# A diffusion-transformer step on one core: expert rows accumulated by DMA in two DRAM tensors, the last tile placed by TensorE

## Chip, core and metric

The kernel runs on one core of one Trainium2 chip. The metric is device time of one launch in microseconds (us); lower is better. Before the change it is 1660.75 us, the median of three runs (1660.02 to 1660.82).

## What is computed

Two layers of a transformer with shared router, over 640 tokens (128 context, 512 latent) of width 1024, all in float32. Each layer has modulation, a combined input projection, two kinds of attention, merge and output projection, and then a mixture of experts. The change touches the last part and the start of what follows it:

```python
    combine = jnp.sum(jax.nn.one_hot(idx, N_EXPERTS, dtype=jnp.float32) * w[..., None], axis=-2)
    out = jnp.zeros_like(h)
    for e in range(N_EXPERTS):
        hid = jax.nn.silu(h @ w_gate[e]) * (h @ w_up[e])
        out = out + combine[..., e:e + 1] * (hid @ w_down[e])
...
    x = x + gt2 * moe(h2, lp['w_router'], lp['b_router'], lp['w_gate'], lp['w_up'], lp['w_down'])
```

Every token goes to two of the 16 experts (`idx` has two entries), so there are 1280 pairs of token and expert. `gt2` is a row of 1024 values, one for context tokens and one for latent tokens. The next layer begins with an RMS norm of the new `x`.

## The kernel before

**Tiles.** The 1280 expert rows are sorted on the chip into 18 tiles of 128 slots: ten full tiles (one expert each, 128 slots) and eight pair tiles (two experts, 64 slots each). Slots that get no row stay empty, and a pair tile may be empty altogether. The order is fixed in `SCHED` (L67 to L70): tiles 0 and 1 are full, then pair and full tiles alternate (2 is a pair, 3 full, and so on), 15 and 16 are full and 17 is the last pair tile.

**One tile.** TensorE (PE) multiplies the gathered rows with the gate and up weights (`gate_up`, L2200), ScalarE (ACT) applies silu, VectorE (DVE) makes `hid` (L1758), PE transposes it and multiplies it with the down weights into two PSUM banks (`down`, L2233). `ys` (L1170 on ACT, L1724 on DVE) scales one bank each by the slot's routing weight into `ysb`, of which there are two buffers. The loop over tiles is software-pipelined: on PE `gate_up(n)`, then the transposes of the rows of n+1, then `down(n-1)`, then the transposes of `hid` of n. Full tiles from 2 on are computed in three passes, for which ACT makes `hi` and DVE `lo` parts of weights and rows (L1161, L1715, L1720). `gate_up(n+1)` waits for `hid(n)` and, in a full tile, for both `lo` parts of its rows.

**Queues.** SP issues the loads of full tiles' weights. GpSimd (POOL) issues, in one fixed order and into one software queue, the gathers of rows (`xg`, L795), the weights of pair tiles (`gu_a`, `gu_b` with 2 MB each, L804; `dn_a`, `dn_b` with 512 KB each, L811) and the scatter of results (`store_rows`, L827): each slot of `ysb` goes to its own row of `ye_d` in DRAM, 1280 rows, empty slots being skipped (`oob_is_err=False`). `ys(n)` waits until the store of tile n-2 has landed (`y_stored`, L1728), since it writes the same buffer.

**After the last tile.** `load_back` (L604) waits for all stores, then loads for each token tile the two rows of every token (`Y1`, `Y2`); `x` and the gate rows `gt` have been loaded before that (`rows_return`, L591). DVE does three passes of 128x1024 per token tile (L1357, L1361, L1365): sum of the two, times gate, plus `x`. At the end of the kernel each tile is stored to `y_out` (L672). Between the layers the same passes alternate with the norm of the next layer (L1389 to L1398): mean square, inverse root, then PE transposes, ACT and DVE modulate and split (`head_evac`, `head_half`, `head_lo`), and PE starts its first projection tile by tile. PE runs 13 matmuls without a use (`keep_busy`, L1986, L1988) around that point.

Of the kernel before, what the change touches and what calls it, by code (L numbers as in the profile page):

```python
# [24 lines left out]
P = 128  # L25
D = 1024
# [111 lines left out]
def program(nc, w_stream, w_gu, w_dn, x_in, c_cols, params, b_mod2, vecs, g_norm2, da_kc, da_vc, na_kc, na_vc, na_bias,  # L138
            w_router, b_router, consts, rc_in, tok_in, rope, y_out, dk_out, dv_out, nk_out, nv_out):
    nc.disable_value_cache = True  # L140
    ctx = ExitStack()
    with ctx:
# [56 lines left out]
        tok = at("tok", [P, 2 * NT], F32)  # L199
# [112 lines left out]
        def in_junk(name, shape, dt, kb):  # L312
# [6 lines left out]
        row_t = in_junk("row_t", [P, 2 * NT, MOE_TILES], F16, 1)  # L319
        w_rest = in_junk("w_rest", [P, 2 * NT], F32, 1.75)  # L320
        w_tab = [in_hi("w_tab0", [P, 2 * NT, MOE_TILES], F16, 16), in_hi("w_tab1", [P, 2 * NT, MOE_TILES], F16, 16.5),
                 in_junk("w_tab2", [P, 2 * NT, MOE_TILES], F16, 0.5)]
# [17 lines left out]
        ye_d = nc.dram_tensor("ye_d", [2 * NT * P, D], F32, kind="Internal").ap()  # L340
# [122 lines left out]
        inv_ready = Signal("inv_ready", 1)  # L463
        etab_ready = Signal("etab_ready", 1)
        eidx_ready = Signal("eidx_ready", 1)
# [11 lines left out]
        y_act = Signal("y_act", MOE_TILES)  # L477
        y_dve = Signal("y_dve", MOE_TILES)
        y_stored = [Signal(f"y_stored{b}", half[b], 0, 16) for b in range(2)]
        gathered = [Signal(f"gathered{t}", 5 if t == 0 else 3, 0, 16) for t in range(NT)]  # L480
# [27 lines left out]
        s_out = sem("out_stored")  # L508
# [45 lines left out]
        def _(sp):  # L554
# [9 lines left out]
            for l in range(DEPTH):  # L564
# [26 lines left out]
                def rows_return(l):  # L591
                    for k in range(MU):
                        sp.wait_ge(*unit_used(l, N_FULL - 2, k))
                    sp.wait_ge(dn_used.sem, dn_used.at(l, N_PAIR - 2))
                    sp.wait_ge(x_parked.sem, x_parked.at(l, 0))
                    sp.wait_ge(mod_stored.sem, mod_stored.at(l, 3))
                    for t in range(NT):
                        sp.dma_start(x[:, t, :], x_spill[:, t, :]).then_inc(gathered[t].sem, 16)
                        if t == 0:
                            for cond in range(2):  # L600
                                sp.dma_start(gt[:, cond, :], mod_d[l, cond, 5 * D:6 * D].partition_broadcast(P)
                                             ).then_inc(gathered[0].sem, 16)
# [9 lines left out]
                for u in range(NU):  # L612
# [3 lines left out]
                    if l >= 1 and u == 3:  # L616
                        rows_return(l - 1)
# [1785 lines left out]
```

## Time and profile before

| what | value |
|---|---|
| runs timed without the profiler | 1660.02, 1660.75, 1660.82 us |
| profiled execution, first to last instruction (span) | 1665.8 us |
| PE busy | 1550.5 us, 93% of the span |
| DVE busy | 899.4 us, 54% |
| ACT busy | 700.1 us, 42% |
| POOL busy | 297.8 us, 18% |
| mean granted TensorE clock | 0.974 of full speed |
| chain that ended last | 81% PE, 8% DMA, 6% DVE |
| moved by DMA | 337.55 MB, mean 203 GB/s |

The profiled execution has only its span as a time of its own; it is 5.05 us longer than the median of the three runs. A busy share is an average over stages with different limits. The expert stage runs from about 622 to 825 us in the first layer and from about 1435 to 1636 us in the second; the tail after it ends at 1665.8 us.

### The profile page before, as it was taken

The numbers are of one execution on the slowest core, as the hardware profiler recorded it, in microseconds if no ns is written. First come the engines' busy times: TensorE is split into PE (matmuls) and PEld (weight loads), VectorE is DVE, ScalarE is ACT, GpSimd is POOL, SyncE is SP. The second block draws the span as 40 slices with busy tenths as digits, with TensorE's granted clock in tenths as the row PEclk, the third lists the DMA queues.
The fourth block names the chain that finished last, engine by engine and source line by source line (L and its number), as shares of the span: only waits on it lengthen the run. The fifth ranks groups of instructions, "written<-read, shape, count | busy, mean of one in ns | idle before, by whom it ended". The sixth has DMA issues, their size and how long they took to land.

```text
span 1665.8 us, 21787 instructions
## 1 busy us (share of the span) xinstructions
PE 1550.5 (93%) x8180; PEld 1107.1 (66%) x8180; DVE 899.4 (54%) x1723; ACT 700.1 (42%) x1335; POOL 297.8 (18%) x321
## 2 busy tenths in 40 slices
PE   4999999999999989999779999999999999899992
PEld 1777777777787855554456777777777888555561
DVE  1566664455554752455575656543455556344554
ACT  4543554445521313444553455534454132144550
POOL 1001000011101014565200010000111010345640
PEclk9999999999999989999989999999999999999996
DMA  8541205534365379999847212353345253898847
GB/s 339 205 153 58 77 26 189 185 109 161 111 234 219 135 278 400 383 401 346 303 178 270 95 39 77 120 185 126 114 152 204 87 202 127 308 414 336 331 143 286
DMA packets 92376, 337.55 MB, mean 203 GB/s; under 512 B 20960, under 2 KB 21024, under 8 KB 89328
## 3 DMA queue, kind: packets, MB, share of 16 engines
q1 hardware_dynamic: 53136, 197.68, 32.5%
q0 software_dynamic: 38992, 135.86, 22.1%
q10 hardware_dynamic: 144, 2.62, 0.4%
q8 instruction: 65, 1.06, 0.3%
q14 instruction: 39, 0.32, 0.1%
HBM read 351.22 MB, written 47.35 MB: 239 GB/s over the span
## 4 chain that ended last, share of the span: by engine, by line
PE 81%; DMA 8%; DVE 6%; ACT 2%; issue 2%; SPq 1%; POOL 0%; POOLq 0%; ACTq 0%; DVEq 0%
PE ps L1884 16%; PE ps L1886 16%; PE ps L1885 16%; PE ps L2214 6%; PE ps L1876 5%; DMA gu_b<-w_gu,eidx 4%; PE ps L2263 3%; PE ps L2036 3%; PE ps L2018 2%; PE ps L1843 2%; PE ps L1792 2%; PE ps L2096 2%; PE ps L2197 2%; PE ps L2230 2%; PE ps L2070 1%
## 5 line engine op out<-in xcount | busy, mean ns | idle before, releaser
L1884 PE MATMUL ps<-hi,hT_hi 128*128 128x512 f32 x960 | 392.8, 409 | 5.5 <-ACT o_a L1094 3.0
L1886 PE MATMUL ps<-hi,hT_lo 128*128 128x512 f32 x960 | 377.1, 393 | 0.0
L1885 PE MATMUL ps<-lo,hT_hi 128*128 128x512 f32 x960 | 376.3, 392 | 0.0
L1884 PEld LDWEIGHTS ps<-hi,hT_hi 128*128 128x128 f32 x960 | 181.8, 189 | 64.8 <-issue 23.6
L1886 PEld LDWEIGHTS ps<-hi,hT_lo 128*128 128x128 f32 x960 | 181.4, 189 | 40.1
L1885 PEld LDWEIGHTS ps<-lo,hT_hi 128*128 128x128 f32 x960 | 182.2, 190 | 32.4
L890 ACT ACTIVATE hi<-raw 128x1024 fp32r<-128x1024 f32 x106 | 108.4, 1054 | 136.6 <-DMA raw<-w_stream 136.6
L1236 DVE TENSOR_TENSOR lo<-raw,hi 128x1024 fp32r<-128x1024 f32 x106 | 127.5, 1220 | 65.4 <-ACT hi L890 65.0
L1715 DVE TENSOR_TENSOR lo<-raw,hi 128x1024 fp32r<-128x1024 f32 x96 | 112.7, 1221 | 39.7 <-ACT hi L1161 33.9
L2214 PE MATMUL ps<-gu_a,xT 128*64 128x512 f32 x256 | 116.1, 607 | 6.7 <-DMA gu_b<-w_gu,eidx 6.7
L2214 PE MATMUL ps<-gu_b,xT 128*64 128x512 f32 x256 | 116.1, 607 | 0.0
L1161 ACT ACTIVATE hi<-raw 128x1024 fp32r<-128x1024 f32 x96 | 95.5, 1055 | 5.0 <-PE ps L1886 5.0
L1071 ACT ACTIVATE e_da<-ps,neg_m 128x640 f32<-128x640 f32 (+1 forms) x80 | 55.9, 704 | 73.2 <-DVE neg_m L1493 73.2
L2214 PEld LDWEIGHTS ps<-gu_a,xT 128*64 128x64 f32 x256 | 34.5, 140 | 74.7 <-issue 74.7
L1493 DVE TENSOR_REDUCE neg_m<-ps 128x1 f32<-128x640 f32 (+1 forms) x80 | 53.7, 712 | 54.3 <-PE ps L2025 38.4
L1758 DVE TENSOR_TENSOR hid<-ps,silu_g 128x256 f32<-128x256 f32 x36 | 15.3, 424 | 124.1 <-ACT silu_g L1187 107.0
L1351 DVE TENSOR_REDUCE ssum<-sq 128x8 f32<-128x512 f32 x40 | 27.4, 685 | 78.4 <-ACT stg L988 78.4
L1187 ACT ACTIVATE silu_g<-ps 128x256 f32<-128x256 f32 x36 | 13.8, 383 | 131.0 <-PE ps L1886 58.2
L987 ACT ACTIVATE sq<-ps 128x512 f32<-128x512 f32 x40 | 23.9, 597 | 104.5 <-PE ps L1886 104.5
L927 ACT ACTIVATE pT_na<-ps 128x384 f32<-128x384 f32 (+1 forms) x80 | 31.8, 446 | 77.0 <-PE ps L1876 77.0
L2263 PE MATMUL ps<-dn_a,hidT 128*64 128x512 f32 x128 | 60.0, 612 | 3.2 <-ACT hidT L1195 1.7
L830 POOL DMA_INDIRECT ye_d<-ysb,row_i x36 | 50.7, 1409 | 65.9 <-DVE ysb L1732 57.5
(312 smaller groups left out, 2880.8 us busy)
## 6 DMA issues: line engine op xcount, KB each, us to landing
raw<-w_stream SPq DMA_DIRECT2D x112, 512.0 KB
raw<-w_gu SPq DMA_DIRECT2D x80, 512.0 KB
raw_m<-w_stream SPq DMA_DIRECT2D x68, 512.0 KB, 5.4
raw<-w_dn SPq DMA_DIRECT2D x40, 512.0 KB
bias_na<-na_bias POOLq DMA_DIRECT2D x32, 384.0 KB, 3.4
sg<-sg_d POOLq DMA_DIRECT2D x8, 1280.0 KB, 9.7
y<-ye_d SPq DMA_DIRECT2D x20, 512.0 KB, 5.2
raw_p<-w_stream SPq DMA_DIRECT2D x16, 512.0 KB, 16.0
```

Of the source, the lines that this page charges most:

```text
L890: act.activation(hi[s][:], raw[s][:], ACT.Copy).then_inc(is_hi.sem, 1)
L1071: act.activation(e_da[:, i % 2, m, 0:nk], ps_flat[:, m * 1024:m * 1024 + nk], ACT.Exp, bias=neg_m[:, 2 * (i % 2) + m:2 * (i % 2) + m + 1], ...
L1161: act.activation(hi[k][:], raw[w][:], ACT.Copy).then_inc(is_hi.sem, 1)
L1236: dve.tensor_tensor(lo[s][:], raw[s][:], hi[s][:].bitcast(F32), ALU.subtract).then_inc(is_lo.sem, 1)
L1493: dve.tensor_reduce(neg_m[:, c:c + 1], ps_flat[:, m * 1024:m * 1024 + nk], AX.X, ALU.max, negate=True).then_inc(mx_done.sem, 1)
L1715: dve.tensor_tensor(lo[w][:], raw[w][:], hi[k][:].bitcast(F32), ALU.subtract).then_inc(is_lo.sem, 1)
L1876: ins = pe.transpose(ps[:, 5 + n % 2, j * P:(j + 1) * P], src, ident[:])
L1884: pe.matmul(out, w_hi, m_hi, start=first, stop=False)
L1885: pe.matmul(out, w_hi, m_lo, start=False, stop=False)
L1886: return pe.matmul(out, w_lo, m_hi, start=False, stop=last)
L2214: ins = pe.matmul(ps[cs, 0, :], xT[:, kc, cs], pair_gu[q % 2][h][:, kc * 512:(kc + 1) * 512], start=(kc == 0), stop=(kc == KC - 1))
L2263: ins = pe.matmul(ps[cs, 2 + c, :], hidT[:, k, cs], pair_dn[q % 2][h][k][:, c * 512:(c + 1) * 512], start=(k == 0), stop=(k == 1))
```

## The change

There are now two DRAM tensors per layer, `acc[l][0]` and `acc[l][1]`, each with 640 token rows and 128 spare rows. The first is filled with `x` (the store that went to `x_spill`), the second with zeros (`zero_in`, five stores from POOL during attention). POOL adds each tile's `ysb` to one of them with an indirect DMA that accumulates (`compute_op=ALU.add`): full tiles in turn to one or the other, a pair tile's first 64 slots to the first and its last 64 to the second. Every add waits until the add before it on the same tensor has landed (`added`). Empty slots are added to spare rows, so each add moves all its rows.

The gate is applied before the add: DVE writes the gate row of each slot into `ysb` (`row_gates`, one pass of 128x1024, placed ahead of `hid(n)` and waiting for the adds of two tiles before), and `ys` multiplies both PSUM banks by weight and gate on DVE (two passes of 128x512). ACT has no part in it. The gate rows are loaded before the expert stage.

The last tile is not added by DMA. DVE builds five 128x128 matrices of zeros and ones (`perm`), PE multiplies each with the last `ysb` (two matmuls per token tile), and DVE adds the two banks to `x`. `load_back` therefore waits for the adds of tiles 0 to 16 alone, and loads `x` and `xb` for each token tile: one DVE pass of 128x1024 and two of 128x512 per token tile instead of three of 128x1024. At the start of the second layer these passes are ordered differently, the 13 matmuls without a use are gone, and the scratch for DMA descriptors is half of its default (`dynamic_dma_scratch_size=8192`), which makes room for the gate rows.

```diff
+LAST = MOE_TILES - 1
+ACC_ROWS = (NT + 1) * P
+ADD_TO = {}
+for _n in range(LAST):
+    ADD_TO[_n, 0] = SCHED[_n][1] % 2 if IS_FULL[_n] else 0
+    if not IS_FULL[_n]:
+        ADD_TO[_n, 1] = 1
+ADD_NO = {key: sum(1 for other in ADD_TO if other < key and ADD_TO[other] == b) for key, b in ADD_TO.items()}
...
-                def rows_return(l):
+                def load_back(l):
                     for k in range(MU):
                         sp.wait_ge(*unit_used(l, N_FULL - 2, k))
...
+                    for b in range(2):
+                        sp.wait_ge(added[b].sem, added[b].at(l, N_ADDS[b] - 1))
                     for t in range(NT):
...
+                        sp.dma_start(x[:, t, :], acc_x[l][:, t, :]).then_inc(x_loaded[t].sem, 16)
+                        sp.dma_start(xb[t][:], acc[l][1][t * P:(t + 1) * P, :]).then_inc(x_loaded[t].sem, 16)
...
-                def store_rows(n):
-                    po.wait_ge(y_act.sem, y_act.at(l, n))
+                def add_part(n, h):
+                    b = ADD_TO[n, h]
+                    if ADD_NO[n, h] >= 1:
+                        po.wait_ge(added[b].sem, added[b].at(l, ADD_NO[n, h] - 1))
+                    rows_at = row_h if h else row_i
+                    p1 = P if IS_FULL[n] else HALF
+                    po.indirect_dma_start(acc[l][b], bass.IndirectOffsetOnAxis(rows_at[0:p1, XD_COL[n]:XD_COL[n] + 1], 0),
+                                          ysb[n % 2][h * HALF:h * HALF + p1, :], None, bounds_check=ACC_ROWS - 1,
+                                          oob_is_err=True, compute_op=ALU.add).then_inc(added[b].sem, 16)
...
-                def ys(n):
+                def row_gates(n):
+
                     if n >= 2:
-                        dve.wait_ge(y_stored[n % 2].sem, y_stored[n % 2].at(l, n // 2 - 1))
+                        for h in range(1 if IS_FULL[n - 2] else 2):
+                            b = ADD_TO[n - 2, h]
+                            dve.wait_ge(added[b].sem, added[b].at(l, ADD_NO[n - 2, h]))
...
+                    return chained(STT(out=ysb[n % 2][:], in0=gtm[:, 0, :], scalar=p_slot[:, c:c + 1], in1=gtm[:, 1, :],
+                                       op0=ALU.mult, op1=ALU.add))
...
+                def ys(n, gated):
+
+                    dve.wait_ge(*down_done(l, n))
+                    after(gated)
...
+                        ins = STT(out=half_row, in0=ps[:, 2 + j, :], scalar=w_slot[:, c:c + 1], in1=half_row, op0=ALU.mult,
+                                  op1=ALU.mult)
...
+                    if n >= 1:
+                        gated = row_gates(n - 1)
                     dve.wait_ge(silu_done.sem, silu_done.at(l, n))
                     dve.tensor_tensor(hid[:], ps[:, 0, D_EXP:2 * D_EXP], silu_g[:], ALU.mult).then_inc(hid_done.sem, 1)
...
+                def last_rows(l, t):
+                    dve.wait_ge(x_loaded[t].sem, x_loaded[t].at(l, 1))
+                    after(chained(dve.tensor_tensor(x[:, t, :], x[:, t, :], xb[t][:], ALU.add)))
+                    dve.wait_ge(pm_done.sem, pm_done.at(l, t))
+                    for j in range(2):
+                        half_row = x[:, t, 512 * j:512 * j + 512]
+                        ins = dve.tensor_tensor(half_row, ps[:, PERM_BANKS[t][j], :], half_row, ALU.add)
+                    ins.then_inc(x_ready.sem, 1)
...
+                    ins = pe.matmul(ps[:, PERM_BANKS[t][j], :], perm[:, t, :], ysb[LAST % 2][:, 512 * j:512 * j + 512],
+                                    start=True, stop=True)
```

**VectorE, tile 4 (a pair tile) and its neighbours, before.** `ysb_93` is the buffer of odd tiles, the first row of the fence is `hid` of tile 4, and `y_stored1` counts landed stores of odd tiles.

```order
L1715 TENSOR_TENSOR lo_59<-raw_58,hi_60 128x1024 [waits w_hi]
L1758 TENSOR_TENSOR hid<-ps,silu_g 128x256 [waits silu_done]
L1720 TENSOR_TENSOR xT_lo<-ps,xT_hi 128x512 [waits xt_act] x2
L1732 TENSOR_SCALAR ysb_93<-ps,w_slot 128x512 [waits y_stored1,w_used11]
L1758 TENSOR_TENSOR hid<-ps,silu_g 128x256 [waits silu_done]
```

**The same place after.** `rows_added0` and `rows_added1` count landed adds on the two tensors.

```order
L1728 TENSOR_TENSOR lo_59<-raw_58,hi_60 128x1024 [waits w_hi]
L1746 SCALAR_TENSOR_TENSOR ysb_95<-gtm,p_slot 128x1024 [waits rows_added1]
L1794 TENSOR_TENSOR hid<-ps,silu_g 128x256 [waits silu_done]
L1733 TENSOR_TENSOR xT_lo<-ps,xT_hi 128x512 [waits xt_act] x2
L1756 SCALAR_TENSOR_TENSOR ysb_95<-ps,w_slot,ysb_95 128x512 [waits dve_chain,w_used11]
L1756 SCALAR_TENSOR_TENSOR ysb_95<-ps,w_slot,ysb_95 128x512
```

The wait for tile 1's result to have left the buffer stood behind `hid` and the two `xT_lo`; now it stands ahead of them.

**GpSimd, from tile 1's result on, before.** The names are those of the text above.

```order
L804 DMA gu_a_240<-w_gu,eidx 128x4096 [waits pair_gu_used]
L830 DMA ye_d<-ysb_93,row_i 1280x1024 [waits y_dve,y_act]
L795 DMA xg_250<-h_d,inv_i 128x1024 [waits xt_done]
L811 DMA dn_b_70<-w_dn,eidx 128x1024 [waits pair_dn_used]
L830 DMA ye_d<-ysb_251,row_i 1280x1024 [waits y_dve,y_act]
L804 DMA gu_b_241<-w_gu,eidx 128x4096 [waits pair_gu_used]
```

**The same place after.**

```order
L815 DMA gu_a_251<-w_gu,eidx 128x4096 [waits pair_gu_used]
L844 DMA acc_1<-ysb_95,row_i 768x1024 [waits y_dve]
L806 DMA xg_261<-h_d,inv_i 128x1024 [waits xt_done]
L822 DMA dn_b_70<-w_dn,eidx 128x1024 [waits pair_dn_used]
L844 DMA acc_0<-ysb_262,row_i 768x1024 [waits rows_added0,y_dve]
L844 DMA acc_1<-ysb_262,row_h 768x1024 [waits rows_added1]
L815 DMA gu_b_252<-w_gu,eidx 128x4096 [waits pair_gu_used]
```

Tile 2's result is now two DMAs, and the second waits until tile 1's add has landed; `gu_b` of pair tile 6 stands behind that wait.

## Rows read from the trace of the kernel before

**Rows 1.** The page: busy time of PE, and the chain that ended last

```profile
PE 1550.5 (93%) x8180; PEld 1107.1 (66%) x8180; DVE 899.4 (54%) x1723; ACT 700.1 (42%) x1335; POOL 297.8 (18%) x321
...
PE 81%; DMA 8%; DVE 6%; ACT 2%; issue 2%; SPq 1%; POOL 0%; POOLq 0%; ACTq 0%; DVEq 0%
```

**Rows 2.** Windows (us): busy PE, PEld, DVE, ACT, POOL; granted clock; DMA share; GB/s

```profile
660.00:688.00 28.00, 26.39 (x131) 14.14 (x129) 13.88 (x17) 14.87 (x24) 14.91 (x12) 1.00 1.02 421
1470.00:1505.00 35.00, 31.33 (x145) 17.01 (x145) 14.32 (x18) 15.31 (x24) 16.99 (x15) 0.95 1.02 419
```

**Rows 3.** Timeline of POOL: start, length, instruction, idle before and its releaser

```profile
658.23 1.01 POOL L830 DMA_INDIRECT ye_d<-ysb,row_i  x1 [0.30 <-issue]
...
669.04 1.98 POOL L804 DMA_INDIRECT gu_b<-w_gu,eidx  x1 [0.31 <-issue]
...
1471.03 1.02 POOL L830 DMA_INDIRECT ye_d<-ysb,row_i  x1 [0.30 <-issue]
```

**Rows 4.** Timeline of DVE: `hid` of tile 4 and `ys` of tile 3, both layers

```profile
672.50 0.42 DVE L1758 TENSOR_TENSOR hid<-ps,silu_g 128x256 f32<-128x256 f32 x1
...
678.73 0.75 DVE L1732 TENSOR_SCALAR ysb<-ps,w_slot 128x512 f32<-128x512 f32 x1 [4.16 <-DMA ye_d<-ysb,row_i]
...
1485.25 0.42 DVE L1758 TENSOR_TENSOR hid<-ps,silu_g 128x256 f32<-128x256 f32 x1
...
1492.82 0.75 DVE L1732 TENSOR_SCALAR ysb<-ps,w_slot 128x512 f32<-128x512 f32 x1 [5.49 <-DMA ye_d<-ysb,row_i]
```

**Rows 5.** Timeline of PE: `gate_up` of tiles 5 and 6; then one of PE's waits (second layer)

```profile
675.83 0.48 PE L1884 MATMUL ps<-hi,xT_hi 128*128 128x512 f32 x1
...
688.90 1.08 PE L2214 MATMUL ps<-gu_a,xT 128*64 128x512 f32 x1 [2.51 <-DMA gu_b<-w_gu,eidx]
...
1488.57 0.48 PE L1884 MATMUL ps<-hi,xT_hi 128*128 128x512 f32 x1
...
1504.73 0.61 PE L2214 MATMUL ps<-gu_a,xT 128*64 128x512 f32 x1 [1.78 <-DMA gu_b<-w_gu,eidx]
...
PE ps L2263 <- DMA dn_b<-w_dn,eidx: 1.5, 1, 1.5
```

**Rows 6.** Tiles 10 to 12 of the first layer: DVE and PE timelines

```profile
740.62 0.42 DVE L1758 TENSOR_TENSOR hid<-ps,silu_g 128x256 f32<-128x256 f32 x1
...
743.98 0.75 DVE L1732 TENSOR_SCALAR ysb<-ps,w_slot 128x512 f32<-128x512 f32 x1 [1.28 <-DMA ye_d<-ysb,row_i]
...
756.95 1.09 PE L2214 MATMUL ps<-gu_a,xT 128*64 128x512 f32 x1 [2.42 <-DMA gu_b<-w_gu,eidx]
```

**Rows 7.** A quiet cycle, DVE and PE; lines of DVE with min/median/max ns

```profile
1576.44 0.42 DVE L1758 TENSOR_TENSOR hid<-ps,silu_g 128x256 f32<-128x256 f32 x1
...
1579.76 0.48 PE L1884 MATMUL ps<-hi,xT_hi 128*128 128x512 f32 x1
...
L1289 DVE SCALAR_TENSOR_TENSOR hrow<-x,nr,G x10: 1283/1285/1286, 560.8 to 1401.8; 128x1024 f32<-128x1024 f32 x10
...
L1604 DVE TENSOR_TENSOR x<-x,tmp x20: 691/692/694, 548.8 to 1399.1; 128x512 f32<-128x512 f32 x20
```

**Rows 8.** The chain that ended last, its end, and `ys` of tile 16

```profile
1631.07 0.75 DVE L1732 TENSOR_SCALAR ysb<-ps,w_slot 128x512 f32<-128x512 f32 x1 [2.09 <-PE ps L1886]
...
1637.39 2.10 DMA ye_d<-ysb,row_i
...
1639.92 4.46 DMA y<-ye_d
1644.41 1.24 DVE y L1357
...
1661.54 1.23 DVE x L1365
```

**Rows 9.** DVE between the layers: first row sum and last `hT_lo`

```profile
835.71 1.23 DVE L1357 TENSOR_TENSOR y<-y,y 128x1024 f32<-128x1024 f32 x1 [3.68 <-DMA y<-ye_d]
...
882.37 1.29 DVE L1346 TENSOR_TENSOR hT_lo<-y,hT_hi 128x512 fp32r<-128x512 f32 x2 [0.40 <-ACT hT_hi L972]
```

More of the change, by code:

```diff
@@ L339, in program @@
         sg_d = nc.dram_tensor("sg_d", [len(GATES), NT, P, 512], F32, kind="Internal").ap()
-        ye_d = nc.dram_tensor("ye_d", [2 * NT * P, D], F32, kind="Internal").ap()
+        acc = [[nc.dram_tensor(f"acc{l}_{b}", [ACC_ROWS, D], F32, kind="Internal").ap() for b in range(2)]
+               for l in range(DEPTH)]
+        acc_x = [a[0][0:NT * P, :].rearrange("(t p) d -> p t d", p=P) for a in acc]
         ps = ctx.enter_context(nc.psum_tensor("ps", [P, 8, 512], F32))
@@ L476, in program @@
         ht_lo = Signal("ht_lo", sum(IS_SPLIT))
[L477 to L480, printed above, removed]
+        y_dve = Signal("y_dve", LAST + 3)
+        added = [Signal(f"rows_added{b}", N_ADDS[b], 0, 16) for b in range(2)]
+        settled = Signal("acc_zeroed", NT, 0, 16)
+        gtm_loaded = Signal("gtm_loaded", 2, 0, 16)
+        pm_done = Signal("pm_done", NT)
+        x_loaded = [Signal(f"x_loaded{t}", 2, 0, 16) for t in range(NT)]
         x_ready = Signal("x_ready", NT)
@@ L642, in _ @@
                 head_pair(3)
+                sp.wait_ge(mod_stored.sem, mod_stored.at(l, 3))
+                for cond in range(2):
+                    sp.dma_start(gtm[:, cond, :], mod_d[l, cond, 5 * D:6 * D].partition_broadcast(P)
+                                 ).then_inc(gtm_loaded.sem, 16)
                 def weights(j, units):
@@ L671, in _ @@
                 sp.wait_ge(x_ready.sem, x_ready.at(DEPTH - 1, t))
-                sp.dma_start(y_out[:, t, :], x[:, t, :]).then_inc(s_out, 16)
-            sp.wait_ge(s_out, 16 * NT)
+                sp.dma_start(y_out[:, t, :], x[:, t, :]).then_inc(x_parked.sem, 16)
+            sp.wait_ge(x_parked.sem, x_parked.layer * DEPTH + 16 * NT)
         @blk.gpsimd
@@ L734, in _ @@
                     store_gate(g)
+                    if 2 <= g < 2 + NT:
+                        r0 = (g - 2) * P
+                        po.dma_start(acc[l][1][r0:r0 + P, :], zero_in).then_inc(settled.sem, 16)
                 po.wait_ge(kv_out.sem, kv_out.at(l, 1))
@@ L1751, in _ @@
                     head_rows(l + 1)
+                dve.wait_ge(gtm_loaded.sem, gtm_loaded.at(l, 1))
+                after(chained(TT(gtm[:, 0, :], gtm[:, 0, :], gtm[:, 1, :], ALU.subtract)))
                 for n in range(MOE_TILES):
@@ L1778, in _ @@
                             next_lo(w)
-                ys(MOE_TILES - 1)
+                ys(LAST, row_gates(LAST))
                 if l + 1 < DEPTH:
@@ L1965, in head_unit @@
                 def head_unit(k, t):
+                    if k == 0 and t < 2 and l >= 1:
+                        pe.wait_ge(x_ready.sem, x_ready.at(l - 1, 3 + t))
                     if k == 0:
```

174 lines of the change are left out of this document (92 added, 82 removed).

## Prediction

> **What bounds the kernel.** I read the page first: PE is busy for 93% of the span and makes up 81% of the chain that ended last, so time moves only where PE waits or has nothing left to do [rows 1]. Then the windows of the expert stage, for what stands beside PE: from 660 to 688 us and from 1470 to 1505 us the DMA share is 1.02 at 421 and 419 GB/s, so the DMA engines are full while PE is just fed [rows 2]. Then the timelines around the full stretches. There PE does wait: 2.51 us for `gu_b` of tile 6 in the first layer, 1.78 us in the second, 2.42 us for that of tile 12 [rows 5, 6]. Last the end of the chain: from the last `ysb` to the end PE has no part [rows 8]. So there are two places to win, after each layer's last tile, and one to lose, the full stretches of the expert stage.
>
> **The tail, removed and put in its place.** Before, the last row sum ends at 1661.54+1.23=1662.77 us. After, `load_back` hangs on tile 16. Its `ys` begins at 1631.07 us [rows 8] and is now two passes of 0.69 us [rows 7], so it ends at 1632.5; the store before was issued 0.85 us after its `ysb` (1635.79+0.75 to 1637.39), so the add goes out at 1633.4. How long an accumulating DMA takes no row shows for 512 KB; the plain store took 2.10 us in quiet [rows 8]; it could take up to twice that with a read of the target, and I take 3. SP and the first loads take 0.43+4.46 us as before: DVE begins at 1641.3. Each token tile costs 1.24+2x0.69=2.62 us instead of three passes of 1.24 [rows 7, 8], five of them 13.1: 1654.4 us. That is 8.4 us less; I take **-8**, bounds -4 (loads and stores in each other's way) and -10. PE's ten placing matmuls hide behind the loads: the last tile's two passes of `ys` end near 1637.7. What is late next is DVE itself.
>
> **Between the layers.** From the first row sum (835.71) to the last `hT_lo` (883.66) [rows 9] it is a chain of DVE and ACT per tile. Starting about 3 us earlier, as in the tail, and saving 1.1 us per token tile helps; but three tiles' sums now stand ahead of the first `head_half` and two more around the first `head_lo`, and without the 13 filler matmuls PE starts its projection at the low clock (after the wait at 688.90 a matmul took 1.08 us against 0.61 after that at 1504.73) [rows 5]. Followed through in the new order I get `hT_lo` of tile 1 some 2 us later than before and of tile 4 some 2 us earlier: **-1.5**, bounds -4 and +2.
>
> **The wait ahead of `hid`.** This is the dear part. Tile 1's store was issued at 658.23 and 1471.03 [rows 3] and had landed only when `ys(3)` could start, at 678.73 and 1492.82 [rows 4]: 20.5 and 21.8 us in the queue, behind a `gu_a` of 2 MB and other weights. Before, that held up only a `ysb` that nobody needed soon; `hid(4)` had run at 672.50 and 1485.25 [rows 4]. In the new order `row_gates(3)` waits for the same landing ahead of `hid(4)`, and PE needs `hid(4)` and then the `lo` rows for `gate_up(5)`, which began at 675.83 and 1488.57 [rows 5]. On top, the adds of tiles 0 and 1 move more: whole tiles instead of filled slots, and a read of the target for each write. At the least nothing more, at the most some 1.5 MB for the two (2x1.05 MB less the filled part of 2x0.5 MB); over 421 GB/s that is 3.6 us, at half that rate 7. I take 3.6. First layer: landed 682.3, row gates 1.28 [rows 7], `hid` 0.42, `xT_lo` about 1.5: `gate_up(5)` at 685.5, 9.7 late. PE was ready for `gate_up(6)` at 688.90-2.51=686.39 [rows 5]; it is ready at 696.1 now, 7.2 us after it began before: **+7** (bounds +3.5 with no extra landing time, +10.5). Second layer: 1496.4+3.2=1499.6, 11 late; ready before at 1502.95, after a wait for `dn_b` of 1.5 [rows 5] that is swallowed too: 1512.5 against 1504.73: **+8** (+4 to +11.5).
>
> **Tiles 10 to 12.** The same pattern, but looser: `ys(9)` could start at 743.98 after `hid(10)` at 740.62, and PE waited 2.42 us for `gu_b` at 756.95 [rows 6]. With 3.6 us more in the queue and that wait swallowed, **+2** (0 to +7). In the second layer no PE wait stood there: **+1** (0 to +4).
>
> **POOL's queue.** The second add of tile 2 waits for tile 1's add, and `gu_b` for tile 6 stands behind it: issued at 669.04 before [rows 3], now not before 683. The queue is then nearly empty, so 2 MB at half to all of 421 GB/s need 5 to 10 us: it lands at 688 to 693, under the new `gate_up(6)` at 696. I cost it at nothing; its cover is the lateness of `hid(4)` itself. Without that it would cost up to 4 us.
>
> **DVE in quiet cycles.** `hid` of a pair tile ran right behind five `lo` passes (1576.44) and `gate_up` of the next full tile began at 1579.76 [rows 7]. Two passes more ahead of it (1.28 and 0.64) push `hid` to 1578.4 and the end of `xT_lo` to 1580.2: 0.4 us. Some five such places outside the full stretches and two where full tiles follow each other: **+2** (0 to +6). ACT's `ysb` of 0.69 us goes, hidden before as well. Gate and zero loads (1 MB and 2.5 MB per layer) lie in attention and mid-layer: nothing (up to +1).
>
> **Sum.** -8-1.5+7+8+2+1+2=+10.5 us on the profiled 1665.8, that is 1676.3. The runs stand 5.05 us under the profile's span, so 1660.75+10.5, **1671 us**.
>
> **A rule against the trace.** The row says 20.5 us for a store of at most 512 KB [rows 3, 4]. The Trainium skill (DMA: Bandwidth & Descriptors, Anatomy of one DMA) puts a DMA at about 2.0 us plus bytes over 436 GB/s: an estimate of 3.2 us for 512 KB. It speaks of one DMA with no queue ahead. The row decides where engines are full.
>
> **Rivals.** *The adds are there in time* (faster): `row_gates(3)` never waits, because the adds leave the queue some 9 us sooner than the stores did. For it: in quiet the store took 2.10 us [rows 8], and SP's loads might yield. Against it: the same `gu_a` is ahead in the same queue, POOL issues it at the same moment. It decides from a landing before about 673 us: then only the gains and a little DVE are left, -8-1.5+2, and some 2 us of `gu_b` waits: **1655**. By the rule above it would come out so. Chance 0.28. *The adds saturate the stage*: 17 tiles of 0.52 MB, read and written, less 1280 rows of 4 KB are up to 12.6 MB more per layer, 30 us at 421 GB/s [rows 2]; if quiet cycles absorb only a third of it, 20 us per layer instead of the 10 above: **1691**, with `gu_b` waits at tiles 6 and 12. For it: the DMA share is already 1.02; against it: PE waited only 2 us for data in such a stretch. Chance 0.12. *The tail gives nothing*: the add of tile 16 takes over 8 us, then DVE begins no earlier than before and saves only 5 passes' difference (5.5 us) less 1: **1675**. For it: nobody has seen an accumulating DMA of this size here; against it: the engines have little else to move by then. Chance 0.08. *Even* (the expert stage loses just what the tail wins): 0.05. The forecast itself: 0.47.
>
> **Numbers.** Range 1651 to 1690: it takes in the fast rival, the bounds of the sum that are not all met at once (-10-4+3.5+4 at the low end, +10.5+11.5+7+4+6 at the high one), and stops just short of the saturated case. The three runs lie within 0.8 us; 0.2% (3.3 us) is what a measurement can tell from no change. Faster 0.28, same 0.09 (low ends of the forecast), slower 0.63.
>
> **What would show it.** `hid(4)` behind a wait for a DMA on `acc` in both layers and PE idle before `gate_up(5)`, 5 to 11 us; `gu_b` issued some 14 us later; the last DVE pass at about 8 us less behind the last `down`; a dip of the granted clock near 680 and 1490. Wrong it would be if the add of tile 1 lands within 15 us of its issue, or if PE's busy share in the expert stage does not fall.

## The result, and the profile after

The changed kernel takes **1713.62 us** (median of four runs, 1711.47 to 1713.99), the kernel before beside it 1660.78 us (four runs, 1660.02 to 1662.26): ratio **1.0311**, 95% interval 1.0285 to 1.0337. It is 52.8 us slower. The forecast was 10.5 us slower, with a range up to 1690. The direction was right, the size was not. The profiled execution has a span of 1711.7 us against 1665.8.

The page of the changed kernel, its first line, the chain that ended last, and the three groups that changed most (busy us, mean ns | idle us of the engine ahead, and what ended it):

```profile
PE 1578.2 (92%) x8194; PEld 1116.7 (65%) x8194; DVE 956.4 (56%) x1815; ACT 679.2 (40%) x1299; POOL 336.7 (20%) x343
...
PE 68%; DMA 17%; DVE 6%; issue 4%; POOL 2%; SPq 1%; ACT 1%; POOLq 0%; DVEq 0%; ACTq 0%
...
L844 POOL DMA_INDIRECT acc<-ysb,row_i x34 | 66.4, 1953 | 97.7 <-DMA acc<-ysb,row_i 64.5 <-DVE ysb L1756 27.0 <-issue 6.1
...
L1746 DVE SCALAR_TENSOR_TENSOR ysb<-gtm,p_slot 128x1024 f32<-128x1024 f32 x36 | 46.3, 1285 | 112.9 <-DMA acc<-ysb,row_i 74.1 <-DMA acc<-ysb,row_h 38.7
...
L844 POOL DMA_INDIRECT acc<-ysb,row_h x14 | 23.4, 1673 | 50.7 <-DMA acc<-ysb,row_i 47.4 <-issue 2.1 <-PE ps L2277 1.1
```

Against [rows 1], DMA's share of the chain went from 8% to 17% and PE's from 81% to 68%. DVE waits 112.9 us ahead of `row_gates`, and POOL 64.5+47.4=111.9 us ahead of an add, each time for an earlier add. The windows, columns as in [rows 2], with one more, from 700 to 820 us of the first layer (in it `hid` of tiles 6 to 14 after, of tiles 7 to 17 before); after:

```profile
660.00:688.00 28.00, 19.53 (x89) 9.89 (x88) 14.21 (x17) 9.38 (x14) 8.71 (x7) 0.86 1.01 356
700.00:820.00 120.00, 103.49 (x472) 58.07 (x469) 67.50 (x79) 43.01 (x65) 61.31 (x47) 0.94 0.97 316
```

and the second of them before:

```profile
700.00:820.00 120.00, 117.58 (x562) 68.41 (x562) 58.99 (x70) 56.24 (x85) 58.99 (x46) 0.99 0.94 355
```

This is the reading that matters most. From 660 to 688 us the DMA engines are as full as before (1.01 against 1.02 in [rows 2]), but move 356 GB/s, not 421. From 700 to 820 us they are fuller than before and move 11% less. The two windows don't hold the same tiles, so this alone is a hint and no more: an add seems to occupy the engines for longer than the bytes that the profile counts for it. The run with plain writes (e1, below) has 412 GB/s at the same share of 1.02 from 660 to 688 us, and 347 at 0.94 from 700 to 820.

DVE's timeline after: `row_gates` of tiles 2, 3, 7 and 9, with `hid` of tiles 3, 4, 6 and 12 of the first layer:

```profile
663.95 1.28 DVE L1746 SCALAR_TENSOR_TENSOR ysb<-gtm,p_slot 128x1024 f32<-128x1024 f32 x1 [7.81 <-DMA acc<-ysb,row_i]
665.15 0.42 DVE L1794 TENSOR_TENSOR hid<-ps,silu_g 128x256 f32<-128x256 f32 x1
...
682.50 1.28 DVE L1746 SCALAR_TENSOR_TENSOR ysb<-gtm,p_slot 128x1024 f32<-128x1024 f32 x1 [8.48 <-DMA acc<-ysb,row_i]
683.70 0.42 DVE L1794 TENSOR_TENSOR hid<-ps,silu_g 128x256 f32<-128x256 f32 x1
...
709.01 0.42 DVE L1794 TENSOR_TENSOR hid<-ps,silu_g 128x256 f32<-128x256 f32 x1
...
732.02 1.28 DVE L1746 SCALAR_TENSOR_TENSOR ysb<-gtm,p_slot 128x1024 f32<-128x1024 f32 x1 [3.50 <-DMA acc<-ysb,row_i]
...
763.62 1.28 DVE L1746 SCALAR_TENSOR_TENSOR ysb<-gtm,p_slot 128x1024 f32<-128x1024 f32 x1 [9.52 <-DMA acc<-ysb,row_i]
...
792.77 0.42 DVE L1794 TENSOR_TENSOR hid<-ps,silu_g 128x256 f32<-128x256 f32 x1
```

and in the second layer `row_gates` of tiles 3 and 5, and PE at `gate_up` of tiles 5 and 6:

```profile
1523.39 1.28 DVE L1746 SCALAR_TENSOR_TENSOR ysb<-gtm,p_slot 128x1024 f32<-128x1024 f32 x1 [8.59 <-DMA acc<-ysb,row_i]
...
1548.78 1.28 DVE L1746 SCALAR_TENSOR_TENSOR ysb<-gtm,p_slot 128x1024 f32<-128x1024 f32 x1 [3.05 <-DMA acc<-ysb,row_i]
...
1526.26 0.79 PE L1944 MATMUL ps<-hi,xT_hi 128*128 128x512 f32 x1 [0.51 <-DVE xT_lo L1733]
...
1538.49 0.64 PE L2277 MATMUL ps<-gu_a,xT 128*64 128x512 f32 x1
```

POOL's timeline after: the adds of tiles 1 and 2, `gu_b` of tile 6, and a wait much later:

```profile
658.55 1.62 POOL L844 DMA_INDIRECT acc<-ysb,row_i  x1 [0.30 <-issue]
...
668.84 2.00 POOL L844 DMA_INDIRECT acc<-ysb,row_i  x1 [1.28 <-DVE ysb L1756]
683.34 1.74 POOL L844 DMA_INDIRECT acc<-ysb,row_h  x1 [12.51 <-DMA acc<-ysb,row_i]
685.38 1.05 POOL L815 DMA_INDIRECT gu_b<-w_gu,eidx  x1 [0.30 <-issue]
...
764.45 1.79 POOL L844 DMA_INDIRECT acc<-ysb,row_i  x1 [16.11 <-DMA acc<-ysb,row_i]
```

And PE at tile 4's transposes of `hid` and at `gate_up` of tile 5:

```profile
684.18 0.69 PE L2333 MATMUL ps<-ident,hid 128*128 128x128 f32 x2 [7.30 <-DVE hid L1794]
685.38 0.79 PE L1944 MATMUL ps<-hi,xT_hi 128*128 128x512 f32 x1 [0.51 <-DVE xT_lo L1733]
```

Up to here, in the first layer, the forecast holds to a fraction of a microsecond: tile 1's add landed when `row_gates(3)` could start, 682.50 (forecast 682.3), `gate_up(5)` began at 685.38 (685.5), `gu_b` was issued at 685.38 (not before 683). What it did not see is the rest of the list, and in the second layer its size was not met step by step (see the part on why).

Where the 45.9 us between the two profiled spans lie, from the starts of `hid` and the ends of the last `ysb` in both traces (us; forecast in brackets):

| stretch | first layer | second layer |
|---|---|---|
| `hid` of tile 0 to `hid` of tile 6 | 68.4 to 79.5: +11.1 (+7) | 69.6 to 77.7: +8.1 (+8) |
| `hid` of tile 6 to `hid` of tile 12 | 68.2 to 83.8: **+15.6** (+2) | 64.2 to 75.6: **+11.4** (+1) |
| `hid` of tile 12 to the last `ysb` | 60.8 to 66.2: +5.4 | 60.1 to 61.1: +1.0 |
| last `ysb` to `hid` 0 of the next layer, or to the end | 615.9 to 613.3: -2.6 (-1.5) | 29.3 to 25.1: -4.2 (-8) |

(+0.1 lies ahead of the first row; the +2 for DVE in quiet cycles belongs to no single stretch.) The tail after, timeline and chain of waits:

```profile
1682.19 1.66 POOL L844 DMA_INDIRECT acc<-ysb,row_i  x1 [7.14 <-DVE ysb L1756]
...
1688.43 0.33 SPq L616 DMA_DIRECT2D x<-acc  x1
...
1693.54 1.23 DVE L1366 TENSOR_TENSOR x<-x,xb 128x1024 f32<-128x1024 f32 x1 [6.92 <-DMA xb<-acc]
...
1705.09 1.23 DVE L1366 TENSOR_TENSOR x<-x,xb 128x1024 f32<-128x1024 f32 x1 [1.18 <-DMA xb<-acc]
```

```profile
1682.19 6.16 DMA acc<-ysb,row_i
1693.23 11.84 DMA xb<-acc
```

With PE nearly done and no weights left to load, the add of one full tile still takes 6.16 us from issue to landing.

### The profile page after: what moved, and what is told of

Same layout as the page of the kernel before. It is cut to its first block, busy times and chain, and to the rows that moved or that the text cites. A ratio compares the mean times of both kernels' runs of the same rounds, so it can differ in the third digit from the quotient of the medians.

```text
span 1711.7 us, 21853 instructions
## 1 busy us (share of the span) xinstructions
PE 1578.2 (92%) x8194; PEld 1116.7 (65%) x8194; DVE 956.4 (56%) x1815; ACT 679.2 (40%) x1299; POOL 336.7 (20%) x343
## 3 DMA queue, kind: packets, MB, share of 16 engines
q0 software_dynamic: 39248, 148.44, 26.8%
HBM read 351.22 MB, written 51.54 MB: 235 GB/s over the span
## 4 chain that ended last, share of the span: by engine, by line
PE 68%; DMA 17%; DVE 6%; issue 4%; POOL 2%; SPq 1%; ACT 1%; POOLq 0%; DVEq 0%; ACTq 0%
PE ps L1944 15%; PE ps L1946 14%; PE ps L1945 14%; DMA acc<-ysb,row_i 12%; PE ps L1936 5%; PE ps L2099 2%; PE ps L2277 2%; PE ps L2081 2%; PE ps L1903 2%; PE ps L2159 2%; PE ps L2293 2%; PE ps L1852 2%; DMA raw_m<-w_stream 2%; PE ps L2133 1%; DMA raw<-w_stream 1%
## 5 line engine op out<-in xcount | busy, mean ns | idle before, releaser
L1944 PEld LDWEIGHTS ps<-hi,hT_hi 128*128 128x128 f32 x960 | 182.2, 190 | 66.2 <-issue 25.4
L1746 DVE SCALAR_TENSOR_TENSOR ysb<-gtm,p_slot 128x1024 f32<-128x1024 f32 x36 | 46.3, 1285 | 112.9 <-DMA acc<-ysb,row_i 74.1
L844 POOL DMA_INDIRECT acc<-ysb,row_i x34 | 66.4, 1953 | 97.7 <-DMA acc<-ysb,row_i 64.5
L1756 DVE SCALAR_TENSOR_TENSOR ysb<-ps,w_slot,ysb 128x512 f32<-128x512 f32 x72 | 50.6, 746 | 24.9 <-PE ps L2317 10.8
L1944 PE MATMUL ps<-hi,xT_hi 128*128 128x512 f32 x128 | 56.5, 441 | 7.6 <-DVE xT_lo L1733 7.6
```

Of the source, the lines that this page charges most:

```text
L844: po.indirect_dma_start(acc[l][b], bass.IndirectOffsetOnAxis(rows_at[0:p1, XD_COL[n]:XD_COL[n] + 1], 0), ysb[n % 2][h * HALF:h * HALF + p1 ...
L1944: pe.matmul(out, w_hi, m_hi, start=first, stop=False)
```

## The experiments

Every ratio is to the kernel before, run on the same chip beside it, with its 95% interval. Chips differed in how much their runs spread; at a ratio of 0.001 to 1.7 us, differences below about 4 us between two runs are not told apart. The edits are to the changed kernel where nothing else is said.

| run | ratio | interval |
|---|---|---|
| changed kernel | 1.0311 | 1.0285 to 1.0337 |
| gates behind `hid` (e2) | 1.0268 | 1.0235 to 1.0300 |
| empty slots skipped (e4) | 1.0245 | 1.0228 to 1.0262 |
| a tensor for each add (e3) | 1.0210 | 1.0188 to 1.0232 |
| plain writes (e1) | 1.0135 | 1.0118 to 1.0152 |
| plain, gates behind (e14) | 1.0128 | 1.0104 to 1.0152 |
| plain, own tensors (e13) | 1.0081 | 1.0051 to 1.0111 |
| plain, own tensors, gates behind (e11) | 1.0021 | 1.0005 to 1.0038 |
| the same with empty slots skipped (e6) | 0.9988 | 0.9969 to 1.0006 |
| e6 with adds (e7) | 1.0086 | 1.0057 to 1.0115 |
| before, scatter made to add (e9) | 1.0142 | 1.0117 to 1.0168 |
| before, wait ahead of `hid` (e5) | 1.0032 | 1.0012 to 1.0053 |
| before, gated (e8, again e12) | 0.9969, 0.9983 | 0.9950 to 0.9987, 0.9967 to 1.0000 |
| before, gated ahead of `hid` (e10) | 1.0025 | 1.0009 to 1.0040 |

**Four suspects, one at a time.** First, what an add costs the engines.

```diff
-                                          oob_is_err=True, compute_op=ALU.add).then_inc(added[b].sem, 16)
+                                          oob_is_err=True).then_inc(added[b].sem, 16)
```

> Every add of an expert tile becomes a plain indirect write of the same rows to the same places (the sum over the two experts of a token is left out; waits, order and bytes written stay). Two theories. Engine time: an accumulating row costs the DMA engines more than a written row, which is why their share stood at 0.96 to 0.99 through the whole expert stage at only 299 to 342 GB/s in the windows from 700 to 820 us, where the kernel before moved 327 to 382 GB/s. Then the time falls to 1665 to 1685 us, the POOL waits for acc (97.7 us in total) fall by half or more, and GB/s in these windows rises above 350. Wait position: what costs is that row_gates stands ahead of hid and waits for whatever lies in the queue, and that each DMA waits for the one before on its tensor. A write stays as long in the queue as an add, and the time stays at 1698 to 1712 us.

1.0135, 1681.92 us: 1.76% of 1661 us or 29 us gone with one argument, as the engine-time theory has it. Its tail shows the price alone. DMA queues (packets, MB, share of 16 engines) from 1675 to 1712 us of the changed kernel, with two adds of full tiles on q0, and loads and stores on q1:

```profile
q1 hardware_dynamic: 2160, 7.87, 55.3%
q0 software_dynamic: 288, 1.05, 18.1%
```

and from 1648 to 1681 us of the plain run:

```profile
q1 hardware_dynamic: 2160, 7.87, 62.5%
q0 software_dynamic: 203, 0.70, 5.3%
```

0.181x37=6.7 us for 1.05 MB is 6.4 us per MB; plain, 0.053x33=1.75 us for 0.70 MB is 2.5, and q1 moves its MB in 2.6 in both. Over the whole span the extra is smaller: the q0 rows of the two pages, 26.8% of 1711.7 us and 24.1% of 1680.8, differ by 54 us, 3.0 us per MB over the plain write for 17.8 MB of adds. **An accumulated byte occupies the DMA engines 2.1 to 2.6 times as long as a written one,** by this and the pairs of runs below (5.2 to 6.4 us per MB against 2.5). A read of the target counted as bytes would make it twice. Not all came as expected: POOL's wait for earlier writes fell only from 111.9 to 88.1 us (not by half), and the windows rose to 347 GB/s (not above 350). So a chain of plain writes waits too.

```diff
-                    if n >= 1:
-                        gated = row_gates(n - 1)
                     dve.wait_ge(silu_done.sem, silu_done.at(l, n))
...
-                        ys(n - 1, gated)
+                        ys(n - 1, row_gates(n - 1))
```

> row_gates(n-1) moves behind hid(n) and both xT_lo, right ahead of ys(n-1), the place at which the kernel before waited for its store. Adds, their bytes and POOL's order stay. Wait position: hid never waits for an add, PE's waits for hid and xT_lo (19.3 and 4.4 us in the first layer, 11.9 and 3.1 in the second) go, and of 53 us over the kernel before some 35 to 45 go: 1668 to 1680 us. Engine time: hid comes early, but gu_b, dn and xg come late from full engines and from POOL's waits; PE then waits for gu_b instead: 1698 to 1710 us.

1.0268: only 7 us, with intervals that leave 0 to 14. The trace shows where the wait went. PE's waits in the changed kernel (us in total, times, longest):

```profile
PE ps L2333 <- DVE hid L1794: 31.1, 12, 7.3
...
PE ps L2277 <- DMA gu_b<-w_gu,eidx: 3.6, 2, 2.1
```

and with the gates behind `hid`:

```profile
PE ps L2275 <- DMA gu_b<-w_gu,eidx: 21.7, 6, 5.0
...
PE ps L2258 <- DMA xg<-h_d,inv_i: 10.6, 4, 4.0
```

The wait for `hid` is gone, and PE waits for weights and rows in its place: these were late all the while, hidden under the late `hid`. My position theory falls as the main cause.

```diff
-                    if ADD_NO[n, h] >= 1:
-                        po.wait_ge(added[b].sem, added[b].at(l, ADD_NO[n, h] - 1))
...
-                    po.indirect_dma_start(acc[l][b], bass.IndirectOffsetOnAxis(...
+                    po.indirect_dma_start(own[l, (n, h)], bass.IndirectOffsetOnAxis(...
```

> Every add goes to a DRAM tensor of its own, so that no add waits for another on POOL (the sum over the tensors is left out: only two of them are loaded back). Every add still accumulates and moves the same rows, and row_gates still waits ahead of hid for the adds of two tiles before. If the chain of adds on POOL is a large part (12.5 us of wait ahead of the second add of tile 2, 16.1 us once later, with gu_b, dn and xg behind it), the time falls to 1680 to 1695 us. If it only fills POOL's time while the engines are full anyway, 1703 to 1714 us.

1.0210, 17 us gone: the chain is a large part, and the time at the upper end of what was expected. (In this run the landings are counted by even and odd tiles, as each tensor gets only one add.) The chain itself is needed where adds meet on a row. The Trainium skill (DMA: Bandwidth & Descriptors, Rules for kernel authors) says that nothing holds the bytes between the read and the write of an accumulating DMA, so an add must wait for the semaphore of the one before. No run here tried it without.

```diff
-...bounds_check=ACC_ROWS - 1,
-                                          oob_is_err=True, compute_op=ALU.add)
+...bounds_check=NT * P - 1,
+                                          oob_is_err=False, compute_op=ALU.add)
```

> Empty slots are skipped instead of added to spare rows: of 17 x 128 = 2176 rows per layer at least 896 less move, 3.67 MB written and read again. Engine time: the adds lose two fifths of their rows, and of the 53 us some 15 to 25 go: 1688 to 1700 us. Wait position: the time in the queue is set by the weights ahead; 1703 to 1713 us.

1.0245, 11 us: 7.73 MB of adds less, somewhat under the 15 to 25 us. The q0 rows of the page were 26.8% of 1711.7 us with all slots and 24.4% of 1698.6 without: 44.3 us of engine time, 5.7 us per MB, between the 5.5 of the pages and the 6.4 of the tail. The sum is unchanged by this edit.

**All at once, and adding put back.** The next run has the four edits together.

> The changed kernel with all four suspects taken away at once: plain writes, empty slots skipped, a tensor for each write (no chain on POOL), row_gates behind hid and xT_lo (left out: the sum of the experts but for two of the tensors). What stays of the change is the gate on DVE, the zero and gate loads and the last tile placed by TensorE. If these four are the whole loss, this is the kernel before less the gain after the last tiles (4 to 8 us) plus up to 2 us of DVE: 1651 to 1660 us. If something else costs (gate passes on DVE in quiet cycles, the smaller scratch for descriptors), it stays above 1665 us.

0.9988, 1660.34 us, the upper end of what was expected. These four are the whole net loss, but not all that the expert stage loses. By the traces (one of each kernel), stretch by stretch, this run spends 8.6 us more than the kernel before from `hid` of tile 0 to the last `ysb` in the first layer and 0.4 in the second; it is 7.1 us shorter between the layers and 6.2 in the tail. What the 9 us are was not tested; the gate passes on DVE are not enough to explain them, as the gated kernel below has them too and is 1.4 and 2.2 us shorter there than the kernel before. With `compute_op=ALU.add` put back (the sum over tensors left out as there):

> As the run with all four suspects taken away, but each write accumulates again; the two differ by nothing else. From the queue's busy share, 17.8 MB of adds took 53.7 us more of all 16 engines than the same rows written plainly (0.268 x 1711.7 less 0.241 x 1680.8), 3.0 us per MB; about 9.5 MB are left here, so 28 us more of engine time. Engine time: the stage before had room only in its second half (DMA share 0.98 to 1.02 in the first), so a third to two thirds of it lands on the path: 10 to 20 us over the plain one. If accumulating costs only through waits in wrong places, these are gone: within 4 us of the plain one.

1.0086: 0.0098 or 16 us over the plain one, inside the 10 to 20, with every wait in a good place and no padding. q0 is 24.5% of 1672.1 us here and 23.0% of 1662.2 there, 27 us more for 10.1 MB of adds (17.8 less 7.7, not the 9.5 expected): 2.7 us per MB more. The padding alone, e11 below against e6 (24.1% of 1667.2 us), gives 2.5 us per MB for plain writes. What stays is the price of adding itself.

The cleanest form of this is the kernel before with one argument more:

```diff
-                                          oob_is_err=False).then_inc(y_stored[n % 2].sem, 16)
+                                          oob_is_err=False, compute_op=ALU.add).then_inc(y_stored[n % 2].sem, 16)
```

> The kernel before with its scatter made to accumulate (compute_op=ALU.add) into its own 1280 rows, same rows, same order, same waits; the rows are filled once in the first layer's attention, ten stores of 512 KB (the values added to are left in the result, so the sum of the experts is not the reference's). 10.5 MB of adds at 3.0 us of engine time more per MB are 31 us. Engine time as the cause: the two runs before, which differ by adding alone, with 9.5 MB lay 15 us apart, so here +13 to +22 us, 1674 to 1682 us, with the waits of PE for gu_b, dn_b and xg grown. If adding costs only in the new order of the changed kernel: within 4 us of the kernel before.

1.0142, 24 us; just over the expected end of 22. The ten fills cost nothing on the path: `hid` of tile 0 began at 629.21 us, before at 629.38. q0 of this run, then of the kernel before:

```profile
q0 software_dynamic: 40432, 141.12, 24.4%
```

```profile
q0 software_dynamic: 38992, 135.86, 22.1%
```

0.244x1686.3=411.5 us less 0.221x1665.8=368.1 are 43.3; the ten fills of 5.24 MB at 421 GB/s take an estimated 12.4 of it, so 10.5 MB of adds cost 31 us more of engine time, 2.9 us per MB. PE's waits for `xg` went from 0.9 to 7.8 us.

**The place of the wait.** First in the kernel before:

```diff
+                    if n >= 3:
+                        dve.wait_ge(y_stored[(n - 1) % 2].sem, y_stored[(n - 1) % 2].at(l, (n - 1) // 2 - 1))
                     dve.wait_ge(silu_done.sem, silu_done.at(l, n))
                     dve.tensor_tensor(hid[:], ps[:, 0, D_EXP:2 * D_EXP], silu_g[:], ALU.mult)...
```

> The kernel before with one wait moved: DVE waits for the store of tile n-3 ahead of hid(n), where row_gates(n-1) stands in the changed kernel, and not ahead of ys(n-1). No instruction and no byte is added. This is the step of the prediction by itself (+3.5 us and +4 us without any extra landing time, for tile 4 in each layer). If the position is what costs, even with plain stores: 1667 to 1680 us, with hid(3), hid(4) or hid(11) late. If plain stores land in time nearly everywhere, so that it takes the slow adds to make the position dear: 1660 to 1666 us.

1.0032, 5 us (2 to 9), on the border between the two theories. `hid` of tile 4 in both layers of this run, against 672.50 and 1485.25 in [rows 4]:

```profile
676.87 0.42 DVE L1760 TENSOR_TENSOR hid<-ps,silu_g 128x256 f32<-128x256 f32 x1 [5.07 <-DMA ye_d<-ysb,row_i]
...
1490.38 0.42 DVE L1760 TENSOR_TENSOR hid<-ps,silu_g 128x256 f32<-128x256 f32 x1 [4.87 <-DMA ye_d<-ysb,row_i]
```

`hid(4)` is late by 4.4 and 5.1 us even with a plain store, the mechanism of the forecast; yet `hid` of tile 6 comes at 698.15 against 697.80, since the wait for `gu_b` behind it took the delay in (PE waits 1.1 us for `gu_b` in this whole run, 6.7 us before). The gated kernel, below, with the gate pass ahead of `hid`:

> The kernel with the gate in each tile and the plain scatter, its gate pass moved ahead of hid(n), together with the wait for the store of tile n-3 that it needs: the place where the changed kernel has it. No byte more. Position as a cause of its own: +4 to +9 us over the gated kernel (the moved wait in the kernel before gave +0.3%), with hid(4) late by some 4 to 5 us in both layers. If the position only matters with slow adds: within 2 us of the gated kernel.

1.0025 against 0.9983 for the gated kernel in the same set of runs: 7 us. So the place alone costs a few us with plain stores too.

**Padding rows, and chain against place, in plain writes.**

> The run without the four suspects, with one given back: empty slots are written to spare rows again, so all 2176 rows per layer move (plain writes, a tensor for each, row_gates behind hid; the sum is left out but for two tensors). 7.7 MB more in the two layers are 18 us at 421 GB/s; if the expert stage takes in between a third and two thirds of it: 6 to 12 us over the run without the four. If bytes hide: within 3 us of it.

1.0021, 5.5 us over e6, just under the expected band.

> The run with plain writes (1.0135 of the kernel before), with a tensor for each write, so that no write waits for another on POOL; row_gates still stands ahead of hid (left out: the sum but for two tensors). Between that run and the one that also has row_gates behind hid (1.0021) lie 19 us. Position moved by itself cost 5 to 7 us in plain kernels, so the chain on POOL should be some 12 us of it: 1.0060 to 1.0080, that is 1.0075 less 2 to 4 us either way. If the position is the larger part: above 1.0100.

> The run with plain writes with row_gates behind hid and xT_lo; the chain of writes on POOL stays (left out: the sum over the two experts of a token). If the chain is some 12 of the 19 us: 1.0085 to 1.0105. If the position is most: below 1.0060. If each alone hides the other's wait (both stand for the same late landing), both runs come out near 1.0135 or both near 1.0021.

1.0081 and 1.0128. From plain writes (1.0135), taking the chain away gives 9 us, moving the gates nothing that can be measured (1 us), both together 19 us. The chain hides the place: with it, something else is late anyway. The reverse holds too, but less: taking the chain away gives 9 us with the gates ahead and 18 with them behind (1.0128 less 1.0021). POOL in e14, at tile 2, with [rows 3] for comparison (`gu_b` at 669.04), and PE's waits for these weights in the whole run (us in total, times, longest):

```profile
678.98 1.18 POOL L844 DMA_INDIRECT acc<-ysb,row_h  x1 [10.41 <-DMA acc<-ysb,row_i]
680.46 1.04 POOL L815 DMA_INDIRECT gu_b<-w_gu,eidx  x1 [0.30 <-issue]
...
PE ps L2275 <- DMA gu_b<-w_gu,eidx: 12.6, 5, 5.0
```

**A version a little faster than both.** The kernel before with one part of the change: the gate rows on DVE in each tile, right ahead of `ys`, and two passes per token tile at the end. No adds, no chain, ACT's `ysb` gone, the descriptor scratch 8192 as in the change.

```diff
+                    gated = chained(STT(out=ysb[n % 2][:], in0=gtm[:, 0, :], scalar=p_slot[:, c:c + 1], in1=gtm[:, 1, :],
+                                        op0=ALU.mult, op1=ALU.add))
                     dve.wait_ge(*down_done(l, n))
+                    after(gated)
+                    for j in range(2):
+                        half_row = ysb[n % 2][:, 512 * j:512 * j + 512]
+                        ins = STT(out=half_row, in0=ps[:, 2 + j, :], scalar=w_slot[:, c:c + 1], in1=half_row, op0=ALU.mult,
+                                  op1=ALU.mult)
...
-                    mix_rows(l, t)
-                    return chained(dve.tensor_tensor(Y1[t][:], Y1[t][:], gt[:, GI(t), :], ALU.mult))
+                    return chained(dve.tensor_tensor(Y1[t][:], Y1[t][:], Y2[t][:], ALU.add))
```

> The kernel before with one part of the change alone: the gate is multiplied in on DVE in each tile (row_gates right ahead of ys, behind hid), ACT's ysb goes, the plain scatter to 1280 rows and its two loads per token stay. After the last tile each token tile needs two passes of 1.24 us instead of three. Five passes are 6.2 us in the second layer, a part of that in the first. If the gate passes lie in DVE's idle time (it is busy for 54%): 1651 to 1656 us. If they delay hid or ys by 0.5 to 1 us per tile on the path: 1659 to 1668 us.

> The gated kernel (gate in each tile on DVE behind hid, plain scatter, two passes per token tile at the end) once more, with more rounds, to narrow its interval: 0.9969 of the kernel before, with 0.9950 to 0.9987, if the first result holds; 1.000 if that was the spread of one chip.

0.9969 and, on another chip, 0.9983: some 3 to 5 us faster than before, the first interval clear of 1, the second just touching it. In the profiled run of the first the tail is 3.7 us shorter (25.6 us from the last `ysb` to the end against 29.3). Why not the full 6.2 us: the last two token tiles there, with a wait for a load ahead of the second.

```profile
1645.47 1.22 DVE L1345 TENSOR_TENSOR y<-y,y 128x1024 f32<-128x1024 f32 x1
1646.73 1.22 DVE L1349 TENSOR_TENSOR x<-x,y 128x1024 f32<-128x1024 f32 x1
1648.84 1.23 DVE L1345 TENSOR_TENSOR y<-y,y 128x1024 f32<-128x1024 f32 x1 [0.89 <-DMA y<-ye_d]
```

**The account.** Read upwards in the table: e6 stands 2 us under the kernel before, the padding rows add 5.5 us (e11), chain and place together 19 us (e1), adding instead of writing 29 us (changed kernel). These are differences along one path through the table, so they add up to the whole 51.5 us by construction; along another path the parts come out otherwise. Accumulating alone was worth 16 us in e7 with 10.1 MB of adds, 24 in the kernel before with 10.5 MB, and 29 here, with 17.8 MB: per MB that is 1.6, 2.3 and 1.6 us. At equal bytes it was worth 29 us with chain and place as in the change, 23 with the gates behind (1.0268 less 1.0128) and 21 without the chain (1.0210 less 1.0081). That a chain makes each add dearer is therefore likely, by some 6 to 8 us, but not shown: the four intervals together leave room for no difference.

## Why the prediction was right and wrong

**Right.** The sign; that in both layers `row_gates(3)` waits for tile 1's add ahead of `hid(4)` and costs several us by tile 6 (7 and 8 forecast, 11.1 and 8.1 measured for the whole stretch); the gain between the layers (-1.5, measured -2.6); that `gu_b` of tile 6 goes out late (16 us, forecast some 14) and PE hardly notices (it waited 3.6 us for `gu_b` in all, against 6.7 before). In the first layer the 4.1 us by which +7 was short are two things: `gate_up(6)` began at 698.19 and not at 696.1, after matmuls at the lower clock (the granted clock was 0.86 from 660 to 688 us, 1.00 before), and `row_gates(5)` then waited 2.38 us ahead of `hid(6)`. An earlier wait I had overlooked, 7.81 us at `row_gates(2)`, put `hid(3)` at 665.15 and not at 660.64; `hid(4)` would have waited until 682.50 for tile 1's add in any case.

**Luck: the +8 of the second layer.** Its stretch measured +8.1, but not by the steps of the forecast. Counted from `hid(0)`, which began 29.62 us later than before (1472.25 against 1442.63), tile 1's add landed 1.0 us later than the store had and not 3.6, `gate_up(5)` (at 1526.26) was 8.1 us late and not 11, `gate_up(6)` (at 1538.49) 4.1 and not 7.8. The other 4 us came from `row_gates(5)`, which waited 3.05 us for tile 3's add ahead of `hid(6)`: a wait that the forecast did not have.

**Wrong: the step "Tiles 10 to 12", +2 and +1.** Measured +15.6 and +11.4, and +5.4 and +1.0 behind tile 12. It took the delay for one of two full stretches, with quiet cycles between. There are none after the change: an add needs 6.16 us even in quiet, and each DMA on a tensor waits for the one before, two for a pair tile. In the first layer `row_gates` waits in nearly every tile, and POOL 4 to 16 us ahead of eight adds. The windows told that before's quiet was thin: the DMA share was 0.94 from 700 to 820 us, and I had looked only where it was 1.02.

**Wrong beneath it: what all the adds together cost.** The 3.6 us for the adds of tiles 0 and 1 was right where it was used in the first layer: tile 1's add landed at 682.50, the store before at 678.73, the plain write of e1 at 679.13. But the sum charged such a price only around tile 4 and tiles 10 to 12 of each layer, and nothing for the adds of the other tiles, though each of them occupies the engines. An added byte was priced as two bytes at 421 GB/s, 4.8 us per MB; the runs show 5.2 to 6.4. So the price was a little low, and the number of places that pay it far too small: for the 17.8 MB of adds it is some 54 us of engine time over plain writes, and taking the adding away gave 29 us. The rival "the adds saturate the stage" had this mechanism, and 1691 us, with 20 us lost per layer (measured 32.1 and 20.5); it too priced the adds by bytes, and was given 0.12. It should have been the forecast, at a somewhat higher price and with the chain: the reason I held against it, that PE waited only 2 us for data, says how much slack there was, not how much more would fit.

**"POOL's queue", costed at nothing.** Right for tile 6, where the late `hid` covered it, wrong as a rule for the kernel: taking the chain away was worth 17 us. The cover was itself a delay that I had booked as a cost, and both hang on the same adds; e2 and e14 show that removing the early wait alone leaves PE waiting for weights and rows.

**The tail, -8: measured -4.2.** The add took 6.16 us and not 3, SP and the first loads 5.1 us (1688.43 to 1693.54) as taken, five token tiles 14.1 and not 13.1. The last load was issued at 1693.23 and took 11.84 us, beside the stores of finished tiles; and the last `ysb` has two passes of its own now, 1.41 us where DVE had 0.75. With plain writes and nothing else changed (e1) the write of tile 16 took 3.42 us and the tail 22.0 us, 7.3 less than before: the -8 was nearly right for a plain write.

**The rival "the adds are there in time", and the rule against the trace.** Tile 1's add landed 24 us after its issue (658.55 to 682.50), so this rival, given 0.28, is out. The Trainium skill (DMA: Bandwidth & Descriptors, Anatomy of one DMA) gave an estimate of 3.2 us for 512 KB. By that the plain write of a full tile in the quiet tail agrees (3.42 us), the add (6.16) does not: nothing in the rule tells an add from a copy.

Not tried: POOL's loads ahead of the adds in its order, the smaller descriptor scratch by itself (the gated kernel has it and is not slower than the kernel before), and more than two buffers of `ysb`, for which there was no room.

## What to carry to other kernels

Price a DMA that accumulates by the time it occupies the engines, here 2.1 to 2.6 times a plain write, and charge it for every one of them, not only at the places where the trace before shows a wait. Before moving a sum into DMA, look at the DMA share over the whole stage: here the part that I had taken for quiet already stood at 0.94. Adds into one tensor are a chain: count its links per tile, and everything queued behind each link. And when two waits hang on the same late transfers, take both away before concluding that either is harmless.

## What the runs showed that I had not expected

- An accumulating indirect DMA occupied the DMA engines for 5.2 to 6.4 us per MB, a plain one for 2.5; alone, a full tile took 6.16 us against 3.42 us from issue to landing.
- GpSimd too needs longer to issue it: 1953 ns in the mean against 1352 ns for the same plain write (the 34 DMAs of line 844 with `row_i`); its busy time fell from 336.7 to 305.4 us with that one argument. How much of the price of adding comes onto the path through this, since weight loads stand behind the adds in GpSimd's order, and how much through the DMA engines, no run here separates.
- The byte counts of the queue show nothing of it: 148.44 MB on q0 with adds and with plain writes alike, and 351.22 MB read from HBM in both. If the target is read, that is in the busy share only.
